# Expert stage of a transformer layer: the rows of a short expert run as the lower half of another expert's 64-row block

## What is computed

```python
logits = jnp.dot(t, w_router) + b_router
top_val, top_idx = lax.top_k(logits, TOP_K)          # 4 of 32 experts for each of 1024 tokens
...
def expert_block(args):                              # some rows of one expert e
    idx, e = args
    xb = t[idx]
    hu = xb @ w1[e] + b1[e]                          # 1024 -> 2048
    glu = jnp.minimum(hu[:, 0::2], SWIGLU_LIMIT)
    lin = jnp.clip(hu[:, 1::2], -SWIGLU_LIMIT, SWIGLU_LIMIT)
    act = glu * jax.nn.sigmoid(SWIGLU_ALPHA * glu) * (lin + 1)
    return act @ w2[e] + b2[e]                       # 1024 -> 1024
```

## Time and profile before

| | us |
|---|---|
| median of three runs | 2781.38 |
| the profiled execution, its own time | 2784.06 |
| its span, first to last instruction | 2782.3 |
| a period of one S and one P (two in the middle: 1817.32 to 1914.56, 1914.56 to 2011.78) | 97.24, 97.22 |
| a single pass of the last loop | 35.60 |
| last scatter of expert rows starts at | 2683.14 |

### The profile page before, as it was taken

The page is one execution under the profiler, slowest core; times in us unless marked ns, Lnnn a source line. Parts: engine busy times, 40 slices in busy tenths (PEclk is TensorE's granted clock), DMA queues, the critical chain, the costliest instruction groups (busy, mean ns, idle before and its releaser), DMA issues. The chain is left out here.

```text
span 2782.3 us, 40051 instructions
## 1 busy us (share of the span) xinstructions
PE 2573.8 (93%) x12548; PEld 2021.3 (73%) x12549; DVE 1984.9 (71%) x2844; ACT 1532.7 (55%) x1871; POOL 446.4 (16%) x338
## 2 busy tenths in 40 slices
PE   7999969999969579999999999999999999999972
PEld 2466649999957457777877777787777778788850
DVE  2541337777756567787788778878877887999968
ACT  3210126666653266666566666656766665777741
POOL 1000012212111111021022102101210211222210
PEclk9999979999988789999999999999999999999975
DMA  9641043333242197887788788778878877999977
GB/s 338 152 146 42 1 113 82 78 83 81 59 160 107 46 336 248 292 311 268 268 307 303 247 292 312 273 264 306 304 248 293 312 272 266 363 382 383 384 282 294
DMA packets 299021, 646.82 MB, mean 232 GB/s; under 512 B 12210, under 2 KB 13458, under 8 KB 298818
## 3 DMA queue, kind: packets, MB, share of 16 engines
q1 hardware_dynamic: 279634, 574.57, 60.2%
q0 software_dynamic: 19344, 71.71, 7.3%
HBM read 605.97 MB, written 46.22 MB: 234 GB/s over the span
## 5 line engine op out<-in xcount | busy, mean ns | idle before, releaser
L1607 DVE TENSOR_TENSOR w_lo_x<-wring_x,w_hi_x 128x2048 fp32r<-128x2048 f32 x446 | 1010.8, 2283 | 31.2 <-issue 20.9
L1522 ACT ACTIVATE w_hi_x<-wring_x 128x2048 fp32r<-128x2048 f32 x448 | 852.2, 1908 | 28.8 <-DMA wring_x<-in_w_mlp 27.8
L1754 PE MATMUL psum<-w_hi_x,x_hi_x 128*128 128x512 f32 x1184 | 499.1, 422 | 1.9 <-DVE w_lo_x L1607 1.9
L1756 PE MATMUL psum<-w_hi_x,x_lo_x 128*128 128x512 f32 x1184 | 463.6, 392 | 0.0
L1755 PE MATMUL psum<-w_lo_x,x_hi_x 128*128 128x512 f32 x1184 | 462.9, 391 | 0.0
L1487 POOL TENSOR_TENSOR poolgate_x<-poolgate_x 128x1 f32<-128x1 f32 x74 | 93.4, 1262 | 1283.0 <-DVE y_x L1640 708.1
L1756 PEld LDWEIGHTS psum<-w_hi_x,x_lo_x 128*128 128x128 f32 x1184 | 223.0, 188 | 49.7
L1754 PEld LDWEIGHTS psum<-w_hi_x,x_hi_x 128*128 128x128 f32 x1184 | 225.3, 190 | 41.7 <-DVE w_lo_x L1607 2.4
L1755 PEld LDWEIGHTS psum<-w_lo_x,x_hi_x 128*128 128x128 f32 x1184 | 224.1, 189 | 43.4
L1754 PE MATMUL psum<-w_hi_x,a_hi_x 128*128 128x512 f32 x592 | 234.9, 397 | 0.0
L1756 PE MATMUL psum<-w_hi_x,a_lo_x 128*128 128x512 f32 x592 | 231.0, 390 | 0.0
(11 more groups left out here) (309 smaller groups left out, 4046.0 us busy)
## 6 DMA issues: line engine op xcount, KB each, us to landing
wring_x<-in_w_mlp SPq DMA_DIRECT2D x448, 1024.0 KB, 6.8
bias<-bias_d SPq DMA_DIRECT2D x32, 640.0 KB, 7.8
late<-in_w_ada SPq DMA_DIRECT2D x32, 512.0 KB, 3.7
yg<-y_d SPq DMA_DIRECT2D x8, 2048.0 KB, 10.8
ring<-in_w_ada SPq DMA_DIRECT2D x4, 2048.0 KB, 8.5
ring<-in_w_in SPq DMA_DIRECT2D x4, 2048.0 KB, 9.9
ring<-in_w_out SPq DMA_DIRECT2D x2, 2048.0 KB
mix_d<-o SPq DMA_DIRECT2D x16, 256.0 KB, 2.0
```

The source lines that it names most:

```text
L1522: act.activation(w_hi[:, n % HI, k, :], ring[:, n % RING, k, :], ACT.Copy).then_inc(hi_done, 1)
L1607: dve.tensor_tensor(w_lo[:, n % LO, k, :], ring[:, n % RING, k, :], w_hi[:, n % HI, k, :].bitcast(F32), ALU.subtract).then_inc(lo_done, 1)
L1754: pe.matmul(bank, hi[:, k, :], w_hi[:, n % HI, k, :], start=(not biased and k == 0), stop=False)
L1756: last = pe.matmul(bank, lo[:, k, :], w_hi[:, n % HI, k, :], start=False, stop=(k == KD - 1))
```

## The change

A third kind of pass is added. A triple pass (T in this text, `TRIPLE` in the code) is a pair pass whose 64-row block gets a second, different expert's rows in rows 64 to 127 of `xg`: those of a short expert. The weights of the two experts take turns in the ring: unit 2n is unit n of the long expert, unit 2n+1 is unit n of the short one. Unit 2n serves a full product (r = 0) and a half product (r = 1), as in a pair pass, and unit 2n+1 serves one half product (r = 2) with the short expert's rows. A triple pass has 12 units and 336 matmuls of weights; a single has 6 and 144, a pair 6 and 240.

The upper and lower parts of product r = 2 are added in partitions 64 to 127, so that one clip, one Silu, one multiplication and one transpose serve both halves (their tiles are now 128 partitions, `x_both` and `a_both` twice as wide).

The number of triple passes is worked out in the kernel: the smallest of the pair passes, the short experts, the pair passes less one, and the singles beyond the pairs less one. With 14 pair passes, 6 short experts and 23 singles (short ones among them) that is the smallest of 14, 6, 13 and 8: six. `program` becomes three loops: S and T six times, S and P eight times, S three times. The weights that are loaded stay 37 sets of 12 chunks.

```diff
+            triple, both, single = counts
+            with engine.Fori(0, triple) as b:
+                body(Step(SINGLE, b, b, b), TRIPLE)
+                body(Step(TRIPLE, b + 1, b, b), SINGLE)
+            with engine.Fori(triple, both) as b:
+                body(Step(SINGLE, b, b, triple), PAIR)
+                body(Step(PAIR, b + 1, b, triple), SINGLE)
+            with engine.Fori(both, single) as b:
+                body(Step(SINGLE, b, both, triple), SINGLE)
...
+        def unit_of(st, n, r):
+            return 2 * n + r // 2 if st.kind == TRIPLE else n
...
+            def triple(st, nxt, chosen):
+                for n in range(NU):
+                    if 1 <= n <= UP:
+                        add_up(st, n - 1, 2)
+                        half_gate(st, n - 1)
+                    if n > UP:
+                        add_output(st, n - 1, 2)
+                    wait_products_before(dve, st, n, 0)
+                    ahead(st, nxt, 2 * n + 1, 0)
+                    if 1 <= n <= UP:
+                        columns(st, 2 * n - 1)
+                    if n == UP:
+                        rows(nxt, 0)
+                        select(nxt, chosen)
+                    if n < UP:
+                        gate(st, 2 * n)
+                    ahead(st, nxt, 2 * n + 1, 1)
+                    if n < UP:
+                        columns(st, 2 * n)
+                        add_up(st, n, 1)
+                    else:
+                        add_output(st, n, 1)
+                    wait_products_before(dve, st, n, 2)
+                    ahead(st, nxt, 2 * n + 2, 0)
+                    ahead(st, nxt, 2 * n + 2, 1)
+                add_output(st, NU - 1, 2)
```

```diff
-                    if r == 0:
-                        pe.wait_ge(lo_done, CH * unit + c + 1 + RING * CH)
+                    if r != 1:
+                        pe.wait_ge(lo_done, CH * (NU * st.passes + u) + c + 1 + RING * CH)
...
+                        if r:
+                            pe.matmul(bank, both[:, k, r - 1, :], w_hi[:, u % HI, k, :], start=(not biased and k == 0), stop=False)
+                            last = pe.matmul(bank, both[:, k, r - 1, :], w_lo[:, u % LO, k, :], start=False, stop=(k == KD - 1))
```

More of the change, by code:

```diff
@@ L1428, in low_parts @@
[L1428 to L1438 removed]
+            triple = engine.value_load(K.table[0:1, TRIPLE_COUNT:TRIPLE_COUNT + 1], min_val=1, max_val=E)
@@ new lines, in slots, with gather @@
+            def slots(table, st):
+                if st.kind == SINGLE:
+                    at = nc.s_assert_within(st.s + counts[0], 1, SINGLE_STEPS - 1, skip_runtime_bounds_check_because="the singles and shorts of all experts are fewer than SINGLE_STEPS")
+                    return table[:, bass.ds(2 * at + PAIR_CHUNKS, 1)]
+                return table[:, bass.ds(3 * st.p, 2 * RMAX)].rearrange("p (r two) -> p r two", two=2)[:, :, 0]
+            def gather(st):
+                for r in range(st.R):
+                    rows = rows_in(st, r)
+                    pool.indirect_dma_start(xg[rows, r, :], None, K.h2_d, bass.IndirectOffsetOnAxis(ap=token[rows, r:r + 1], axis=0)).then_inc(gathered, 16)
@@ L1595, in _, with body @@
+            def body(st, kind):
+                (single, pair, triple)[st.kind - 1](st, st.then(kind))
+            program(counts, act, body)
         @block.vector
         def _(dve):
+            counts = step_counts(dve)
             dve.sem_inc(lo_done, RING * CH)
@@ L1679, in _, with ahead @@
+            def ahead(st, nxt, u, c):
+                piece(*((st, u) if u < st.units else (nxt, u - st.units)), c)
+            first = Step(SINGLE, 0, 0, 0)
             rows(first, 0)
@@ L1713, in _, with single @@
-            program(dve, body)
+                piece(first, 0, c)
+            def single(st, nxt, chosen):
+                for n in range(NU):
+                    if 1 <= n <= UP:
+                        gate(st, n - 1)
+                    wait_products_before(dve, st, n, 0)
+                    ahead(st, nxt, n + 1, 0)
+                    if 1 <= n <= UP:
+                        columns(st, n - 1)
+                    if n - UP in range(nxt.R):
+                        rows(nxt, n - UP)
+                    if n == UP:
+                        select(nxt, chosen)
+                    ahead(st, nxt, n + 1, 1)
@@ L1715, in _, with body @@
+            def body(st, kind):
+                nxt = st.then(kind)
+                chosen = experts_of(dve, nxt, counts[0])
+                (single, pair, triple)[st.kind - 1](st, nxt, chosen)
+            program(counts, dve, body)
         @block.tensor
         def _(pe):
+            counts = step_counts(pe)
             pe.sem_inc(prod_done, PROD0)
```

618 lines of the change are left out of this document (349 added, 269 removed).

## The result

The changed kernel takes 2738.33 us, median of four runs (2734.12 to 2750.28), beside 2780.57 us for the kernel before in four runs: the ratio of all runs is 0.9858, 95% interval 0.9823 to 0.9893, 1.4% faster (the two medians alone give 0.9848). The profiled execution took 2738.21 us, its span is 2736.4 us; before it was 2784.06 and 2782.3. So the two profiles differ by 45.9 us, where 47.1 were forecast.

A forecast was written before the change was run, and what follows sets the result against it. PE was taken to set the pace of all passes. 165.0 us added by six triples, 213.6 removed and 1.5 added in routing gave -47.1, hence 2734.3 us as median, range 2704 to 2764; the forecast case had chance 0.58.

The forecast's parts named there:

- Removed: Six single passes leave the last loop (nine become three): 6 x 35.60 = 213.6 us less.
- PE's work in a triple, and the turn of 14.62 us: Third products add 22.8 us of PE work a triple; a turn takes 14.62 us where a pair's was 10.22.
- the walk: One triple turn, followed from r = 1's end by trace distances; PE stalls 0.3 us for the first split.
- Second units: A triple's two second units, without bias: products of 2 x 3.63 us plus stalls of 0.6 and 0.9, 8.8 us.
- The single behind a triple: DVE starts it late, two splits standing ahead: PE waits 0.9 us, and 0.2 more before the first transposes.
- the places come free: Weight ring in a triple: ACT wants each chunk some 11 us after its place frees, landing takes 6.8: hidden.
- Routing: About a dozen more DVE operations of 0.16 to 0.2 us, some lost: +1.5 us, between 0 and 3.
- (1): PE's work only, all splits in time: a triple adds 22.8 us, 2706 us in all; chance 0.20.
- (2): Waits in a triple are twice the forecast's, 9.4 us instead of 4.7: 2762 us; chance 0.12.
- (3): First split not hidden at the seams: PE waits 2.28 us at 12 units, 27.4 a triple, 2878 us; chance 0.07.
- (4): One triple instead of six: -8 us and some routing, 2776 us; chance 0.03.
- The rule on instructions that start in other partitions: DVE's additions at partition 64 lose overlap: 1.1 us a triple, 6.5 in all if unhidden; outside the sum.

The follow-up runs named there:

- swap: In triples DVE makes the long expert's next first split before the addition for r = 1, against the changed kernel: 2731.20 us.
- short_splits: In triples the short expert's splits cover one of four slices, against the changed kernel: 2736.48 us.
- late_less: Changed kernel with DVE's register loads in mid-pass and a quarter of ten weight chunks left out of each first-loop single: 2727.28 us.
- one_triple: Changed kernel with at most one triple pass instead of six: 2776.13 us, ratio 0.9974 to the kernel before.
- late_split: Changed kernel where the first split of the long expert's next unit waits for product r = 2, not r = 1: 2825.93 us.
- less_dma: Changed kernel with a quarter of ten weight chunks left out of each first-loop single: 2739.66 us.

## Why the prediction was right, and where it was off

It gave 2734.3 us, and 2738.3 were measured, inside 2704 to 2764. The forecast case held, not a rival. By its steps:

- **Removed:** right. Of the three gaps in front of and between the late singles' scatters the one between two late singles is 35.60 us; the first (40.48) and the last (31.20) are like those of before (40.36 and 31.20).
- **PE's work in a triple, and the turn of 14.62 us:** right. 1299.29, 1313.90 and 1328.50 are the bias matmuls of r = 0, 14.61 and 14.60 apart. The parts too: 6.20 us for r = 0 with its wait (5.70 + 0.3 + 0.2 transposes), 4.53 for r = 1 (4.52), 3.88 for r = 2. The wait is 0.37 (0.3) three times a triple, and it stands at the seam that the walk named. Swap showed that it hangs on the addition ahead of the split, and short_splits that it doesn't hang on DVE's amount.
- **Second units:** the walk has three stalls here. The one ahead of the first full second product was put at 0.3 (the end of the first units) and measured 0.23. The one ahead of the second was put at 0.9 and measured 0.63: it supposed that the next pass's `x_lo` pushes three steps in a row. The one behind the last was put at 0.6 and stands at the start of the single, where the first full product comes 0.67 us behind its bias in place of 0.04: 0.63. So of the 26.2 a triple, 25.6 were forecast within T and 0.6 at the single. T came to 85.66 in the mean of six, 25.9 over the pair's 59.77.
- **The single behind a triple: this term was mis-sized.** The forecast was 1.1 us of the 1.3, by "two splits stand ahead of it" plus's 2.28 to the next split, and with the 0.6 above it makes 1.9. The kernel before took 37.60 us for a single behind a pair, in the mean of thirteen, the changed one 40.56: 3.0. The second full product comes 2.03 us behind its bias (1377.44 to 1379.47), where 0.9 was forecast, and PE waits 0.55, 0.41 and 0.27 ahead of transposes, where 0.2 was. The 2.28 was carried over as if it were fixed; it held an "issue" of 1.59 us that I hadn't opened, and this part grows with the number of experts to be read (2.40). What then stayed of the single's slack the late weights took: I had set "the places come free" against the triple alone, with 293 GB/s, and not against the single, which had a share of 0.96 before and now carries 0.5 MB more of rows. late_less shows both, and that 38.7 is left without them. Six times (3.0 - 1.9) for the single and six times (25.9 - 25.6) for T are 8.4, the 8.3 us by which this line of the ledger misses.
- **Common code:** the text said that grown single periods would show a cost at something put at nothing. They show a gain: 0.4 us a period. One part is seen: a half product with its transposes takes 4.23 us in a pair, in place of 4.30 in the earlier trace rows, as the multiplication ahead of the transposes waits 0.15 us for Silu and not 0.22. one_triple places it in the common code; which edit does it wasn't tried.
- **Routing:** +1.5 forecast, -1.7 found, and not to be told from the spread of that start.
- **Rivals:** (1) asked for waits of 0.04; they are 0.37, so the period isn't near 120. Swap is the nearest to that rival, made by an edit: 123.3. (2) asked for twice the waits; inside T no, but counted over the period (126.1 for 124.7) a third of the way there. (3) is the late_split kernel: its price in T was forecast at 27.4 for twelve seams; shown are 12.2 for the five of late_split within T; the sign is as said, the point of turn within 1 us. (4) The counts refute it, and one_triple shows what it would have looked like: 2776.13 for "2776", though its stage fell by 12.3 and a late start made up for it.

The rule on instructions that start in other partitions: in swap's rows the addition for r = 1 starts 0.08 us before the end of the split ahead of it (1304.99 + 2.29 = 1307.28), the one for r = 2, at partition 64, 0.03 behind it (1308.12 + 2.29 = 1310.41). In the single behind a triple the clip at partition 0 starts 0.04 behind the split's end (1377.12 + 4.49 = 1381.61), where behind a pair it started 0.08 before it. There the last operation that had read PSUM was the addition at partition 64. By the Trainium skill (VectorE: DVE Perf Modes, section "Two Vector instructions with no wait between them") an instruction is held when its input from a memory starts in another group of 32 partitions than the last input from that memory; that names both cases, and the trace agrees, with 0.11 and 0.12 us each. The prediction had it as "than the last one"; by that shorter form the clip, which stands behind two splits at partition 0, wouldn't be held. It didn't reach PE: the turn is 14.60, as forecast without it.

## What to carry to other kernels

When a pass becomes longer and shares its loop with a short one, look for the cost in the short one: it inherits the lateness of every engine, and it has the least room to catch up. Of each distance copied from the trace ask what it is made of. Here the idle time named "issue" at the start of a loop body was mostly the engine's own reading of registers; it grew with what was read, and moving it to the middle of the pass gave 7.7 us. A split, copy or conversion that the bottleneck wants goes before the steps that wait for another engine, and here an edit that shifts the order was worth more than one that shortens the work (swap 17 us, short_splits none).

## What the runs showed that I had not expected

- Reading an expert's number from SBUF into a register costs DVE 0.6 to 0.9 us: 0.95 us idle with none (0.35 of it for the end of the addition), 1.51 to 1.60 with one, 2.40 with two.
- Two causes hid each other. Taking away one of them gave 0.3 or 0.4 us a period, taking away both 2.0; less_dma alone would have acquitted the DMA engines.
- The DMA engines stood nearly still for about 2.5 us in a pass whose mean share is 0.97. A mean share hides such a lull; the kernel before has one as well, at a share of 0.96, in a single that takes 37.4 us.
- One moved wait put 2.26 to 2.50 us at each of six seams a triple and added 83 us to the stage: 13.9 us for each triple and the single behind it.
